# Differential attention: the two softmax maps mixed on VectorE before the transposes

## The reference

```
q = rope(rms_norm(q, w[0]));  k = rope(rms_norm(k, w[1]))
lam = exp(sum(lq[0]*lq[1])) - exp(sum(lq[2]*lq[3])) + lam_init
for blk in range(S // 128):                       # two blocks of 128 queries
    s = einsum('bqhmd,bkhmd->bhmqk', qb, kb) * 64**-0.5       # m = 0, 1: two maps
    p = softmax(where(causal, s, -inf), axis=-1)
    p = p[:, :, 0] - lam * p[:, :, 1]
    outs.append(einsum('bhqk,bkhe->bqhe', p, vb))
o = rms_norm(concat(outs), subln_w) * (1 - lam_init)
```

## Time and profile before

| what | value |
|---|---|
| time, median of 3 runs | 3848.83 us (3845.8 to 3853.82) |
| span of the profiled execution, first to last instruction | 3846.0 us |
| PE matmul busy | 3693.2 us, 96% of the span |
| DVE busy | 2244.5 us, 58% |
| ACT busy | 1579.0 us, 41% |
| POOL busy | 1114.0 us, 29% |
| mean granted TensorE clock | 0.991 of full |
| differential attention, first to last instruction of its loop (two layers) | about 2382 to 2441 us and 3222 to 3281 us |

### The profile page before, as it was taken

The page is one execution under the profiler, slowest core; times in us unless marked ns, Lnnn a source line. Parts: engine busy times, 40 slices in busy tenths (PEclk is TensorE's granted clock), DMA queues, the critical chain, the costliest instruction groups (busy, mean ns, idle before and its releaser), DMA issues.

```text
span 3846.0 us, 47412 instructions
## 1 busy us (share of the span) xinstructions
PE 3693.2 (96%) x18063; PEld 3007.2 (78%) x18063; DVE 2244.5 (58%) x2281; ACT 1579.0 (41%) x1943; POOL 1114.0 (29%) x574
## 2 busy tenths in 40 slices
PE   8999999999999899999999999999999998999999
PEld 7886888887888668888868786778788785787787
DVE  6665767656666247566756544456664545448554
ACT  4364444454344344444743342234443332234343
POOL 6800848404848007474038000021000001031000
PEclk9999999999999999999999999999999999999999
DMA  8734767545766247675457454221555553312463
GB/s 274 244 102 159 247 201 241 180 148 198 250 203 225 80 143 245 204 248 187 121 194 238 153 184 128 100 77 41 190 184 180 166 176 101 131 34 87 157 207 128
DMA packets 494411, 649.74 MB, mean 169 GB/s; under 512 B 17227, under 2 KB 394594, under 8 KB 494242
## 3 DMA queue, kind: packets, MB, share of 16 engines
q1 hardware_dynamic: 473508, 569.62, 45.5%
q0 software_dynamic: 19584, 75.50, 5.6%
q10 hardware_dynamic: 1150, 2.29, 0.2%
HBM read 646.29 MB, written 1.05 MB: 168 GB/s over the span
## 4 chain that ended last, share of the span: by engine, by line
issue 58%; POOLq 20%; PE 13%; POOL 7%; SPq 1%; DMA 0%; ACT 0%; DVE 0%; DVEq 0%; ACTq 0%
POOLq L616 7%; POOLq L618 6%; POOLq L620 6%; PE bank L1365 3%; PE bank L970 3%; POOL mod_zone L623 2%; POOL modrow L623 2%; PE bank L940 1%; PE bank L1529 1%; PE bank L1540 1%; POOL modrow L605 1%; POOL mod_zone L605 1%; PE bank L947 1%; PE bank L948 1%; PE bank L949 1%
## 5 line engine op out<-in xcount | busy, mean ns | idle before, releaser
L2282 DVE TENSOR_TENSOR wproj_lo<-wproj,wproj_hi 128x2048 fp32r<-128x2048 f32 x252 | 752.6, 3023 | 130.3 <-ACT wproj_hi L1768 130.3
L970 PE MATMUL bank<-wproj_hi,x_hi 128*128 128x512 f32 x2112 | 535.6, 395 | 14.0 <-DVE arena L2386 9.6
L970 PE MATMUL bank<-wproj_lo,x_hi 128*128 128x512 f32 x2112 | 536.5, 397 | 0.0
L970 PE MATMUL bank<-wproj_hi,x_lo 128*128 128x512 f32 x2112 | 522.9, 390 | 0.0
L1817 ACT CAST actT_hi<-bank 128x512 fp32r<-128x512 f32 x132 | 77.5, 587 | 1063.3 <-PE bank L1001 1063.3
L970 PEld LDWEIGHTS bank<-wproj_hi,x_hi 128*128 128x128 f32 x2112 | 394.3, 189 | 110.6 <-issue 24.8
L580 POOL TENSOR_SCALAR rstd<-sumsq 128x1 f32<-128x1 f32 x38 | 7.6, 199 | 1621.0 <-ACT tok L1751 1620.8
L1768 ACT CAST wproj_hi<-wproj 128x2048 fp32r<-128x2048 f32 x252 | 470.2, 1912 | 12.6 <-DMA wproj<-in_ffn_w_gate_up 12.6
L970 PEld LDWEIGHTS bank<-wproj_hi,x_lo 128*128 128x128 f32 x2112 | 396.9, 188 | 82.8
L970 PEld LDWEIGHTS bank<-wproj_lo,x_hi 128*128 128x128 f32 x2112 | 388.2, 188 | 76.8
L2394 DVE TENSOR_TENSOR actT_lo<-bank,actT_hi 128x512 fp32r<-128x512 f32 x132 | 91.3, 692 | 596.4 <-ACT actT_hi L1817 596.4
(11 more groups left out here) (428 smaller groups left out, 5603.2 us busy)
## 6 DMA issues: line engine op xcount, KB each, us to landing
wproj<-in_ffn_w_gate_up SPq DMA_DIRECT2D x336, 512.0 KB, 6.0
wdown<-in_ffn_w_down SPq DMA_DIRECT2D x132, 1024.0 KB, 5.0
wproj<-in_ffn_w_gate SPq DMA_DIRECT2D x84, 512.0 KB, 5.3
wproj<-in_ffn_w_up SPq DMA_DIRECT2D x84, 512.0 KB, 6.3
wproj<-in_w_in SPq DMA_DIRECT2D x40, 1024.0 KB, 7.2
mod_zone<-in_mod_w POOLq DMA_DIRECT2D x36, 1024.0 KB, 5.9
modrow<-in_mod_w POOLq DMA_DIRECT2D x36, 1024.0 KB, 5.9
wproj<-in_sb_w_qkv SPq DMA_DIRECT2D x96, 256.0 KB, 4.4
```

What stands on the lines that cost most here:

```text
L970: last = nc.tensor.matmul(proj_ps[t][:, :], rounded(x_part[of_x](c)[:, toks]), rounded(w_part[of_w][:, c, :]), start=start and c == 0, sto ...
L2282: V.tensor_tensor(rounded(wproj_lo[w.odd][:, cols]), src[:, cols], wproj_hi[w.odd][:, cols], ALU.subtract).then_inc(cols_lo, 1)
```

## The change

`attend("diff")` is replaced on PE, ACT and DVE by a function of its own, `attend_diff`. The two normalised maps are combined in SBUF, `p = p0 / sum0 - lam * p1 / sum1`, and only the combined map is transposed, copied and multiplied with the values.

- PE: `weigh_values` now waits for `df_mixed` (from DVE) in the place of `at_e` (from ACT), makes 3 transposes in place of 6 and 3 matmuls in place of 6. The order of the other steps is as before. The four heads are written out; before, heads 2 and 3 stood in a loop of one turn.
- ACT: `weights` cover only the causal keys, (t+1)*128 wide, and wait for `df_mixed` of the head before. One copy of the transposed map in place of two.
- DVE: a new step `mix` after `logits` and `prepare` k+2, ahead of `outputs`. `outputs` is a copy of 256 columns from PSUM in place of the scaling of 512 and the subtraction; the head's RMS norm is as before.

```diff
 # PE
+def weigh_values(i, k):
+    pe.wait_ge(df_mixed, done + k + 1)
+    if k:
+        pe.wait_ge(df_copied, done + k)
+    for at, (t, kt) in enumerate(((0, 0), (1, 0), (1, 1))):
+        last = nc.tensor.transpose(down_ps[2][:, at * P:(at + 1) * P],
+                                   score[:, 0, t, kt * P:(kt + 1) * P], ident[:, :])
+    last.then_inc(df_turned, 1)
+    pe.wait_ge(df_copied, done + k + 1)
+    pe.wait_ge(at_o, i.n())
...
+    nc.tensor.matmul(aux_ps[:, 0:P], probT[:, 0, 0:P], values[0], start=True, stop=True)
+    nc.tensor.matmul(aux_ps[:, P:SEQ], probT[:, 0, P:2 * P], values[0], start=True, stop=False)
+    nc.tensor.matmul(aux_ps[:, P:SEQ], probT[:, 0, 2 * P:3 * P], values[1], start=False,
+                     stop=True).then_inc(df_values, 1)
...
 # ACT
+def weights(i, k, hd):
+    act.wait_ge(at_l, i.n(2, 1 + hd))
+    if done + k:
+        act.wait_ge(df_mixed, done + k)
+    for t in range(NT):
+        last = nc.scalar.activation(score[:, hd, t, 0:(t + 1) * P], score[:, hd, t, 0:(t + 1) * P], ACT.Exp,
+                                    bias=negmax[:, hd, t:t + 1],
+                                    accum_out=rowsum[:, hd, t:t + 1])
+    last.then_inc(at_e, 1)
+for k in range(pairs):
+    weights(i, k, 0)
+    weights(i, k, 1)
+    if k + ahead < pairs:
+        evac(k + ahead, 0)
+        evac(k + ahead, 1)
+    if k + 1 < pairs:
+        copy_qk(i.plus(1))
+    act.wait_ge(df_turned, done + k + 1)
...
+    nc.scalar.copy(probT[:, 0, :], down_ps[2][:, 0:384]).then_inc(df_copied, 1)
...
 # DVE
+def mix(i):
+    v.wait_ge(at_e, i.n(2, 2))
+    V.reciprocal(rinv[:], rowsum[:])
+    v.drain()
+    V.tensor_scalar(rinv[:, 1], rinv[:, 1], lam[:, layer:layer + 1], None, ALU.mult)
+    v.drain()
+    for t in range(NT):
+        second = score[:, 1, t, 0:(t + 1) * P]
+        V.tensor_scalar(second, second, rinv[:, 1, t:t + 1], None, ALU.mult)
+    v.drain()
+    for t in range(NT):
+        one, second = (score[:, m, t, 0:(t + 1) * P] for m in range(2))
+        last = V.scalar_tensor_tensor(one, one, rinv[:, 0, t:t + 1], second, ALU.mult, ALU.subtract)
+    last.then_inc(df_mixed, 1)
+def outputs(k):
+    v.wait_ge(df_values, done + k + 1)
+    o = aux_ps[:, 0:SEQ].rearrange("p (t d) -> p t d", t=NT)
+    V.tensor_copy(o_head[:, 0], o)
...
+for k in range(pairs):
+    i = Step(n.pair + k)
+    logits(i, k, 0)
+    logits(i, k, 1)
+    if k + ahead < pairs:
+        prepare(i.plus(ahead))
+    mix(i)
+    outputs(k)
```

More of the change, by code:

```diff
@@ L444, in program @@
         ot_turned, ot_copied = sem("ot_turned"), sem("ot_copied")
+        df_mixed, df_turned, df_copied, df_values = (sem(f"diff_{x}") for x in ("mixed", "turned", "copied", "values"))
         vec_in, vec_turned, vec_ready = sem("vec_in"), sem("vec_turned"), sem("vec_ready")
@@ L1321, in attend, with attend_diff, project_pair, turn_pair @@
                     n.sb += pairs
+            def attend_diff(mid):
+                pairs, ahead = H_A, 2
+                done = n.diff
+                def project_pair(i, w, t, mid=None):
+                    if i.s >= 1:
+                        pe.wait_ge(at_ev, i.n(2, -1 + t))
+                    project(w, t, xT, wproj[w.odd][:, 0:KC * 384].rearrange("p (c n) -> p c n", c=KC), KC,
+                            dmas=3, mid=mid, entering=i.s == n.pair)
+                def turn_pair(i):
+                    pe.wait_ge(at_prep, i.n(1, 1 - n.sb))
+                    pe.wait_ge(at_turned, i.n())
+                    for s in range(2):
+                        for t in range(NT):
+                            at = (s * NT + t) * P
+                            last = nc.tensor.transpose(turn_ps[:, at:at + P], qkv[(i.s - n.pair) % 3][:, t, s * P:(s + 1) * P],
+                                                       ident[:, :])
+                    last.then_inc(at_turn, 1)
+                def scores(i, hd):
+                    if hd == 0:
+                        pe.wait_ge(at_turned, i.n(1, 1))
+                    pe.wait_ge(at_l, i.n(2, -1 + hd))
+                    m = qkT[DH * hd:DH * (hd + 1), 0]
+                    for t in range(NT):
+                        last = nc.tensor.matmul(down_ps[hd][:, t * SEQ:(t + 1) * SEQ], m[:, t * P:(t + 1) * P],
+                                                m[:, SEQ:2 * SEQ], start=True, stop=True)
+                    last.then_inc(at_s, 1)
+                def weigh_values(i, k):
[8 more added lines that the diff above has]
+                    pe.wait_ge(at_o, i.n())
+                    values = [qkv[k % 3][:, t, 256:384] for t in range(NT)]
+                    nc.tensor.matmul(aux_ps[:, 0:P], probT[:, 0, 0:P], values[0], start=True, stop=True)
+                    nc.tensor.matmul(aux_ps[:, P:SEQ], probT[:, 0, P:2 * P], values[0], start=True, stop=False)
+                    nc.tensor.matmul(aux_ps[:, P:SEQ], probT[:, 0, 2 * P:3 * P], values[1], start=False,
+                                     stop=True).then_inc(df_values, 1)
+                def hgrn_queries(half):
+                    w = Step(n.load + pairs)
+                    if half == 0:
+                        pe.wait_ge(w_in[w.odd], DMA * (n.landed[w.odd] + 3 * pairs // 2 + 2))
+                        pe.wait_ge(at_ev, Step(n.pair + pairs - 1).n(2, 2))
+                    slot = wproj[w.odd][:, :].rearrange("p (c n) -> p c n", c=KC)
+                    for q in range(2 * half, 2 * half + 2):
+                        for c in range(KC):
+                            last = nc.tensor.matmul(proj_ps[half][:, (q % 2) * SEQ:(q % 2 + 1) * SEQ],
+                                                    slot[:, c, q * P:(q + 1) * P], xT[:, c, :], start=(c == 0),
+                                                    stop=(c == KC - 1))
+                    last.then_inc(proj_done, 1)
+                for k in range(ahead):
+                    project_pair(Step(n.pair + k), Step(n.load + k), 0, mid if k == 0 else None)
+                    project_pair(Step(n.pair + k), Step(n.load + k), 1)
+                turn_pair(Step(n.pair))
+                scores(Step(n.pair), 0)
+                scores(Step(n.pair), 1)
+                for k in range(pairs):
+                    i, w = Step(n.pair + k), Step(n.load + k)
+                    if k + ahead < pairs:
+                        project_pair(i.plus(ahead), w.plus(ahead), 0)
+                        project_pair(i.plus(ahead), w.plus(ahead), 1)
+                    if k + 1 < pairs:
+                        turn_pair(i.plus(1))
+                        if k == pairs - 2:
+                            hgrn_queries(0)
+                        scores(i.plus(1), 0)
+                        scores(i.plus(1), 1)
+                    else:
+                        hgrn_queries(1)
+                    weigh_values(i, k)
+                n.pair += pairs
+                n.diff += pairs
+                n.loaded(pairs, 3)
+                n.loaded(1, 2)
+                n.lin += 1
@@ L1684, in hybrid @@
             def hybrid(l):
-                attend("diff", lambda: turn_x(1, True))
+                attend_diff(lambda: turn_x(1, True))
                 rwkv(l)
@@ L1967, in attend, with attend_diff, evac, copy_qk @@
                     n.sb += pairs
+            def attend_diff():
+                pairs, ahead, done = H_A, 2, n.diff
+                def evac(k, t):
+                    i, w = Step(n.pair + k), Step(n.load + k)
+                    act.wait_ge(proj_done, w.n(2, 1 + t))
+                    if k >= 3:
+                        act.wait_ge(df_values, done + k - 2)
+                    nc.scalar.copy(qkv[k % 3][:, t, 0:384], proj_ps[t][:, 0:384]).then_inc(at_ev, 1)
+                def copy_qk(i):
+                    act.wait_ge(at_turn, i.n(1, 1))
+                    act.wait_ge(at_s, i.n(2))
+                    nc.scalar.copy(qkT[:, 0, :], turn_ps[:, :]).then_inc(at_turned, 1)
+                def weights(i, k, hd):
[7 more added lines that the diff above has]
+                    last.then_inc(at_e, 1)
+                for k in range(ahead):
+                    evac(k, 0)
+                    evac(k, 1)
+                copy_qk(Step(n.pair))
+                for k in range(pairs):
[5 more added lines that the diff above has]
+                        evac(k + ahead, 1)
+                    if k + 1 < pairs:
+                        copy_qk(i.plus(1))
+                    act.wait_ge(df_turned, done + k + 1)
+                    if done + k:
+                        act.wait_ge(df_values, done + k)
+                    nc.scalar.copy(probT[:, 0, :], down_ps[2][:, 0:384]).then_inc(df_copied, 1)
+                n.pair += pairs
+                n.load += pairs
+                n.diff += pairs
             def skip_linear(blocks):
@@ L2153, in hybrid @@
             def hybrid(l):
-                attend("diff")
+                attend_diff()
                 keep(q_raw, proj_ps, range(2))
@@ L2976, in hybrid @@
             def hybrid(l, then):
```

(2 more changed lines are left out.)

51 lines of the change are left out of this document (added).

## The result

| | before | changed |
|---|---|---|
| median of the runs on record with the result | 3850.28 us (4 runs) | 3879.01 us (4 runs, 3877.59 to 3881.58) |
| ratio, with its 95% interval | | 1.0078 (1.0064 to 1.0092) |
| time of the profiled execution | | 3880.07 us |
| its span | 3846.0 us | 3878.3 us |
| its mean granted clock | 0.991 | 0.984 |

The kernel became 0.78% slower, 28.7 us by the medians. The direction was forecast; the size was forecast as 22 and came out near the end of the range, where the second rival stood (3879). The term that was too low is the loss by the clock. A later set of runs of the same two kernels gave a ratio of 1.0084 (1.0069 to 1.0100).

The account below looks back on a forecast made before the run. PE, with a matmul in flight for 96% of the span, was taken as the bound; 16.9 us of waits plus 5.2 of clock made 22.1, added to the 3848.8 median: 3871 us, range 3862 to 3880.

Parts of the forecast that it names:

- the second rival: Also rival 2: clock costs more, slow longer behind each stop and falling again around head 3; 16.9 + 13.2, 3879; chance 0.15.
- the loss by the clock: PE slowed behind two long stops per layer: 1.6 us and 1.0 us, 5.2 in two layers, bounds 0 to 10.
- The place of the mix: On DVE mix k stands behind prepare k+2, so PE's transposes wait: about 7.5 us at heads 0 and 1.
- Two signs: Profile after: PE busy less in the stage by 4 times some 1 us; gap of about 2.1 between mix and outputs.
- The price of the steps: Durations put on DVE's steps per head: mix 1.80 us (bounds 1.5 and 2.2), the new outputs 2.92.
- The chain of waits: From prepare 2 through four heads to RWKV's first matmul: 8.43 us later a layer, 16.9 for both.
- The removed work: PE's transposes and value matmuls for one map instead of two: 0.67 us less a head, 5.4 in eight heads.
- Costed at nothing: ACT's single map copy, GpSimd, PE's removed loop and the end of outputs 3: no delay on PE.
- The third fall: Clock falling around head 3, where PE stops 2 us for mix 3; 1.6 us a layer, not in the main forecast.
- Rival 1: Behind the long stops the clock holds, or what it loses hides: +16.9 us, 3865.7; chance 0.20.
- Rival 3: Mix k is done when PE finishes scores k+1, so it is covered: -5.4 us, 3843.4; chance 0.04.

Follow-up runs that it names:

- wait_alone: Kernel before, plus one wait: PE's transposes of head k wait until DVE has passed prepare k+2; no mix, nothing removed; 3870.6 us, ratio 1.0058.
- mix_first: Changed kernel with one line moved: DVE does mix k right after logits k, ahead of prepare k+2; 3854.7 us, ratio 1.0022.
- fill_to_measure: Changed kernel with 16 matmuls into an unread PSUM bank ahead of PE's wait for the mix of heads 0 and 1 each; 3870.7 us, ratio 1.0053.
- changed_again: The changed kernel unaltered, run again against the kernel before; 3879.3 us, ratio 1.0084.
- fill_last_stop: Changed kernel with 4 matmuls into an unread PSUM bank ahead of PE's wait for the mix of head 3 alone; 3877.3 us, ratio 1.0076.
- logits_ahead: mix_first, with DVE doing the logits of head k+1 ahead of outputs k; 3846.6 us, ratio 0.9998 to the kernel before.
- queries_first_before: Kernel before with PE's hgrn_queries(0) moved ahead of the turn of head 3, nothing else; 3852.8 us, ratio 1.0012.

## Why the prediction was right and where it failed

In short: the wait and its path were forecast as they came, and the term that failed is the loss by the clock. It was put at 5.2 us; the runs show 8.7 inside the two stages, and up to 3.4 more in a place where the forecast had it at nothing.

**The place of the mix: right.** Stops of 7.6 us were forecast as "about 7.5" at heads 0 and 1, 2 at head 3, almost nothing at head 2, and the profile has 7.62, 7.63, none and 1.91 (second layer: 7.63, 8.01, none, 1.90). `wait_alone` and `mix_first` show it from both sides. Two signs that the prediction named are seen only with the clock held up: in `fill_to_measure` PE is busy 48.97 us in the first stage, less two fillings of 7.17, which is 4.3 below the 38.92 of before, and the gap between `mix` and `outputs` is 2.14 us; in the changed kernel PE is busy 39.37 and the gap is 3.21.

**The price of the steps: right, a little low.** The chain of waits was worked out as 8.43 us a layer, 16.9 in all. With the clock held up it is 8.92 and 9.00, 17.9. From the start of `mix` to PE's first transpose I had 1.86; it is 2407.34 - 2405.35 = 1.99. Four of these a layer are the 0.5 us. `outputs` was put at 2.92 and is 2413.42 - 2410.50 = 2.92. That it fits to the hundredth is partly luck, since it was added up from an average over unlike passes. The removed work gave its 0.67 a head, and it was too small to matter.

**Costed at nothing: right.** ACT, GpSimd, the loads and the end of `outputs` 3 don't show up on PE.

**The clock: this step failed, in size.** I charged 1.6 us for the first stop of a layer and 1.0 for the second, 5.2 in all, taking the one fall that the trace of before has at the entrance of the stage as the price of any fall. Measured by `fill_to_measure` it is 4.23 and 4.45 us inside the stage, 8.7 in all, and in the first profile of the changed kernel 1.69 us more a layer in RWKV's first block (12.33 - 10.64). There were two faults. The price was read from a fall in dense projection matmuls behind a stop of 2.5 us; behind stops three times as long the low clock lasted longer (by the mean clocks an estimated 6.2 of 14.80 us, against 3.5 of 19.39 in the second layer of before), though no run tells whether the stop or the work behind it makes that difference. And what comes first behind them is a row of small steps in a chain (transposes, copy, values), 2410.04 - 2407.34 = 2.70 us in place of 1.78, whose delay DVE's chain takes over as well. The third fall was left to rival 2, on the ground that PE was about as thinly used there before without a fall; it came in three of the four layers of the changed kernel's two profiles.

**Sum.** 17.9 + 8.7 + 3.4 = 30.0 us for the profiled execution, against 32.3 between the two spans. The other 2.3 lie outside the stages, and 3.4 of difference are there before the first stage begins (turn of head 1 at 2397.30 against 2393.93). That turn comes anywhere from 2387.98 (`changed_again`) to 2397.94 us (`fill_to_measure`) in these profiles, with no work altered ahead of it, so this part is the spread between executions. Rival 2 (16.9 + 13.2, 3879) was nearly the case that came, with a chance of 0.15; its time fits so well partly by luck, the chain being 1.0 too low and the clock 1.1 too high, and in `changed_again` the third fall is missing in one layer. Rival 1 (the clock holds) is what `fill_to_measure` has in the stages, 17.9 us; its time, 3870.7, lies 5 us above the 3865.7 that the rival names. The sentence of the Trainium skill that I weighed against the trace ("TensorE: Matmul & The Clock Gate", Part 1: the ramp is under 1% of a typical kernel and no count of slow matmuls is to be fitted) is true of this kernel, where 9 to 12 us of 3879 hang on it. Followed to the letter it would have led further from the time, to 16.9 us in place of 22.1: what hangs on the clock is about a third of the effect that was asked for.

Rival 3 named the point from which all turns, `mix` done when scores k+1 are; `mix_first` is that case. Its -5.4 us did not come: the stop ahead of the turn of head 3 was 4.97 us in place of 3.2, and the clock was low behind it.

## What to carry to other kernels

When work is moved onto the engine that runs beside the critical one, look first at what stands ahead of it in that engine's order: 1.9 us of new work cost 9 us a layer in waits because 7.35 us of preparation for a later head stood in front of it. A single line moved took most of that back, and a gain came only when DVE's and PE's orders were both written anew around it. Price a new stop of PE as the stop plus what the clock takes behind it; here that added half of the wait itself inside the stages.

## What the runs showed of the hardware

- Behind stops of PE of 7.6 to 8.0 us the granted clock was at its lower level in all twelve cases that were profiled with the two long stops left open (`changed`, `changed_again`, `fill_last_stop`, two layers each), and in the first layer the work behind the two stops lost 2.6 and 2.1 us. It was low behind the eight stops of 4.5 to 5.1 us too (`wait_alone`, `mix_first`, `logits_ahead`). Behind a stop of 3.2 us it held in both layers of the kernel before; behind stops of 3.1 us in both layers of `queries_first_before` it did not.
- The length of the stop just ahead does not settle it for short ones: small matmuls behind a wait of 1.7 us ran at a mean clock of 0.65 in `queries_first_before` and at 1.00 in the kernel before.
- Matmuls whose results nobody reads, put into a stop without overrunning it, made the kernel 8 us faster (3879.0 to 3870.7); 30 calls in place of 16, 13.2 us in a stop of 7.6, made it 10 us slower.
- A matmul of fp32 with 256 columns stands in the trace as two records of 0.22 us.
